# Sums of squares of two norms computed in the stages that write the residual stream, router logits with the tokens as the moving side, first expert weight splits behind the routing steps

## The reference

```
# first block
h = modulate(rmsnorm(x, norm_mix), sh1, sc1)
x = x + g1 * diff_attention(h, ...)            # ends in  o @ attn_w_out
h = modulate(rmsnorm(x, norm_ffn), sh2, sc2)   # norm 1 of the change
x = x + g2 * hier_moe(h, ...)
x = rmsnorm(x, norm_final)                     # norm 2 of the change
# second block: p = x @ w_in_2, forgetting attention, rwkv mixing, layer norms, PEER experts
```

## Time and profile before

| | us |
|---|---|
| median of 3 runs (lowest, highest) | 2693.97 (2692.8, 2698.87) |
| the profiled execution's own time | 2691.04 |
| its span | 2689.3 |
| busy PE / PEld | 2396.6 (89%) / 1788.0 (66%) |
| busy DVE / ACT / POOL | 1857.1 (69%) / 1045.6 (39%) / 708.1 (26%) |
| TensorE clock granted, mean over the span | 0.944 |

### The profile page before, as it was taken

The page is one execution under the profiler, slowest core; times in us unless marked ns, Lnnn a source line. Parts: engine busy times, 40 slices in busy tenths (PEclk is TensorE's granted clock), DMA queues, the critical chain, the costliest instruction groups (busy, mean ns, idle before and its releaser), DMA issues. The chain is left out here.

```text
span 2689.3 us, 34854 instructions
## 1 busy us (share of the span) xinstructions
PE 2396.6 (89%) x13046; PEld 1788.0 (66%) x13046; DVE 1857.1 (69%) x3303; ACT 1045.6 (39%) x1886; POOL 708.1 (26%) x648
## 2 busy tenths in 40 slices
PE   3999866999996999985889899999999999999991
PEld 2885555888885686653786688887988874444440
DVE  5639554898895322667656369998899976666669
ACT  3238644878874323653114222113877700000000
POOL 0000001213121000030000013445667766444444
PEclk7999977999998998997989999999999999999995
DMA  7943035786874132222003179798999999999997
GB/s 267 292 132 143 26 131 231 294 313 262 317 287 188 48 94 63 59 67 70 3 3 124 56 255 329 266 325 322 404 409 407 405 397 409 409 409 410 409 409 299
DMA packets 242854, 655.37 MB, mean 244 GB/s; under 512 B 25472, under 2 KB 107648, under 8 KB 227200
## 3 DMA queue, kind: packets, MB, share of 16 engines
q1 hardware_dynamic: 160608, 376.28, 38.3%
q0 software_dynamic: 82080, 276.88, 26.6%
HBM read 662.50 MB, written 34.60 MB: 259 GB/s over the span
## 5 line engine op out<-in xcount | busy, mean ns | idle before, releaser
L2658 POOL DMA_INDIRECT sp_rows<-in_u_rows,sp_flat x184 | 225.7, 1227 | 566.2 <-DVE sp_flat L3100 388.5
L285 DVE TENSOR_TENSOR wide_low<-wide_raw,wide_high 128x2048 fp32r<-128x2048 f32 x138 | 312.4, 2290 | 63.9 <-ACT wide_high L278 62.0
L2864 PE MATMUL ps<-raw,tb_made 128*128 128x512 f32 x768 | 335.0, 592 | 0.0
L2834 PE MATMUL ps<-xT,raw 128*128 128x256 f32 x1424 | 319.7, 381 | 0.0
L2834 PEld LDWEIGHTS ps<-xT,raw 128*128 128x128 f32 x1424 | 268.3, 191 | 34.8
L171 DVE TENSOR_TENSOR w_low<-raw,w_high 128x1024 fp32r<-128x1024 f32 x90 | 110.1, 1225 | 249.1 <-ACT w_high L162 248.7
L278 ACT CAST wide_high<-wide_raw 128x2048 fp32r<-128x2048 f32 x138 | 261.6, 1914 | 22.3 <-PE ps L335 16.0
L2864 PEld LDWEIGHTS ps<-raw,tb_made 128*128 128x128 f32 x768 | 145.8, 190 | 183.2 <-issue 183.2
L2667 DVE SCALAR_TENSOR_TENSOR sp_rows<-sp_rows,sp_x 128x1024 f32<-128x1024 f32 x184 | 222.9, 1223 | 21.5 <-DMA sp_rows<-in_u_rows,sp_flat 19.9
L2676 DVE SCALAR_TENSOR_TENSOR sp_x<-sp_rows,sp_coef,sp_x 128x1024 f32<-128x1024 f32 x124 | 158.4, 1286 | 81.3 <-DMA sp_rows<-in_v,sp_flat 79.8
L3000 ACT ACTIVATE pe_root<-pe_root 128x1 f32<-128x1 f32 x4 | 0.8, 203 | 490.2 <-DVE pe_root L3210 490.2
(11 more groups left out here) (522 smaller groups left out, 5151.8 us busy)
## 6 DMA issues: line engine op xcount, KB each, us to landing
wide_raw<-in_w_experts SPq DMA_DIRECT2D x96, 1024.0 KB, 6.8
raw<-in_v SPq DMA_DIRECT2D x96, 512.0 KB, 6.8
raw<-in_u SPq DMA_DIRECT2D x89, 512.0 KB, 6.8
ada_raw<-in_ada_w SPq DMA_DIRECT2D x24, 1024.0 KB, 7.4
raw<-in_w_in SPq DMA_DIRECT2D x42, 512.0 KB, 3.8
raw<-in_peer_w_q SPq DMA_DIRECT2D x32, 512.0 KB, 4.4
tb_ring<-in_v SPq DMA_DIRECT2D x32, 512.0 KB, 6.8
tb_ring<-in_u SPq DMA_DIRECT2D x29, 512.0 KB, 6.8
```

Source lines behind the costliest of these rows:

```text
L285: self.m.nc.vector.tensor_tensor(self.low_of[:, n % self.READY, :], self.raw[:, n % self.RAW, :], self.high_of[:, n % self.READY, :].bitca ...
L2658: self.m.nc.gpsimd.indirect_dma_start(out=self.rows(g), out_offset=None, in_=src, in_offset=bass.IndirectOffsetOnAxis(ap=self.flat[:, tile ...
L2834: last = nc.tensor.matmul(m.ps[:, HID + r % 2, 0:DT], u[:, c, :], m.xT[:, c, 0:DT], start=c == 0, stop=c == KT - 1)
L2864: last = nc.tensor.matmul(m.ps[:, Y + 2 * n + half, :], made[:, r, n * P:(n + 1) * P], v[:, half * T:(half + 1) * T], start=False, stop=r ...
```

## The change

- The squares of `norm_ffn` are made in `head_norm_projection`: after each chunk, ACT squares the new stream tile into `sq`, DVE adds it to the running sum, and PE makes the one product with ones behind the last projection product. DVE's scale and ACT's Ln and Exp (into `m.rstd`) stand at the end of the same block. For the last chunk, ACT squares before it writes its high weight part.
- `rms_norm` for `norm_ffn` is replaced by `ffn_norm`: DVE scales, ACT shifts, and PE multiplies each finished tile with the 20 columns of `router_w` as weights and the 512 tokens as the moving side (8 products instead of 32). ACT copies the logits, [20, 512], to SBUF.
- In `router`, PE turns the logits with 4 transposes instead of computing them. The three splits of expert weights stand behind the routing steps on ACT and DVE, not ahead.
- The squares of `norm_final` are made in `combine`: ACT squares each tile behind DVE's addition, PE sums the eight with ones, and the steps to `m.rstd` follow there. The block `inverse_rms` is gone.

```diff
@@ -543,32 +543,6 @@
                 rest(KT - 1)
 
 
-def inverse_rms(nc, m, name, out):
...
 def project(nc, m, pe, name, high, low, bank_free, chunks=8, n0=0, banks=8):
 
 
@@ -822,6 +796,8 @@
 
     squared, summed, logged, rooted, chain_s, scaled, highs, lows = (m.sem("hn_" + n) for n in (
         "squared", "summed", "logged", "rooted", "chain", "scaled", "highs", "lows"))
+    residual, x_squared, x_added, x_summed, averaged, x_rooted = (m.sem("hn_" + n) for n in (
+        "residual", "x_squared", "x_added", "x_summed", "averaged", "x_rooted"))
     with nc.Block() as block, ExitStack() as mem:
         sb = lambda n, s: mem.enter_context(nc.sbuf_tensor("hn_" + n, s, F32))
         sq, gain, eps = sb("sq", [P, HEADS, T]), sb("gain", [P, 1]), sb("eps", [P, 1])
@@ -853,6 +829,8 @@
                 w = weights(n)
                 for c in range(KT):
                     product(w, n, c)
+            pe.wait_ge(x_added, KT - 1)
+            nc.tensor.matmul(m.ps[:, 0, :], m.ones[:], sq[:, 0, :], start=True, stop=True).then_inc(x_summed, 1)
 
         @block.scalar
         def _(act):
@@ -874,9 +852,19 @@
                 if h >= 1:
                     rounded(h - 1)
             rounded(HEADS - 1)
-            for n in range(KT):
+
+            def square(n):
+                act.wait_ge(residual, n + 1)
+                nc.scalar.activation(sq[:, n, :], m.xT[:, n, :], ACT.Square).then_inc(x_squared, 1)
+
+            for n in range(KT - 1):
                 m.stream.done(act, "attn_out", n)
                 m.stream.high(act, "attn_out", n)
+                square(n)
+            square(KT - 1)
+            m.stream.high(act, "attn_out", KT - 1)
+            act.wait_ge(averaged, 1)
+            inverse_root(nc, act, m.rstd[:], x_rooted, 0)
 
         @block.vector
         def _(dve):
@@ -896,12 +884,54 @@
                 if h >= 1:
                     rest(h - 1)
             rest(HEADS - 1)
+
+            def add_square(n):
+                dve.wait_ge(x_squared, n + 1)
+                if n >= 2:
+                    dve.wait_ge(x_added, n - 1)
+                nc.vector.tensor_tensor(sq[:, 0, :], sq[:, 0, :], sq[:, n, :], ALU.add).then_inc(x_added, 1)
+
             for n in range(KT):
                 m.stream.done(dve, "attn_out", n)
                 nc.vector.scalar_tensor_tensor(out=m.xT[:, n, :], in0=m.ps[:, n, :],
                                                scalar=m.mod[:, 2 * KT + n:2 * KT + n + 1], in1=m.xT[:, n, :],
-                                               op0=ALU.mult, op1=ALU.add)
-                m.stream.low(dve, "attn_out", n)
+                                               op0=ALU.mult, op1=ALU.add).then_inc(residual, 1)
+                if n < KT - 1:
+                    m.stream.low(dve, "attn_out", n)
+                if n >= 1:
+                    add_square(n)
+            m.stream.low(dve, "attn_out", KT - 1)
+            dve.wait_ge(x_summed, 1)
+            nc.vector.tensor_scalar(m.rstd[:], m.ps[:, 0, :], 1.0 / D, EPS, ALU.mult, ALU.add).then_inc(averaged, 1)
+
+
+def ffn_norm(nc, m, h, logits):
+
+
+    scaled, shifted, summed = (m.sem("fn_" + n) for n in ("scaled", "shifted", "summed"))
+    with nc.Block() as block:
+        @block.vector
+        def _(dve):
+            for k in range(KT):
+                nc.vector.scalar_tensor_tensor(out=h[:, k, :], in0=m.xT[:, k, :], scalar=m.norm2[:, k:k + 1], in1=m.rstd[:],
+                                               op0=ALU.mult, op1=ALU.mult).then_inc(scaled, 1)
+
+        @block.scalar
+        def _(act):
+            for k in range(KT):
+                act.wait_ge(scaled, k + 1)
+                nc.scalar.activation(h[:, k, :], h[:, k, :], ACT.Identity, bias=m.mod[:, 3 * KT + k:3 * KT + k + 1]
+                                     ).then_inc(shifted, 1)
+            act.wait_ge(summed, 1)
+            nc.scalar.copy(logits[:], m.ps[0:logits.shape[0], 0, :])
+
+        @block.tensor
+        def _(pe):
+            for k in range(KT):
+                pe.wait_ge(shifted, k + 1)
+                last = nc.tensor.matmul(m.ps[0:logits.shape[0], 0, :], m.router_w[:, k, :], h[:, k, :], start=k == 0,
+                                        stop=k == KT - 1)
+            last.then_inc(summed, 1)
 
 
 def first_of_equals(nc, link, out, eq, seen, width):
@@ -912,7 +942,7 @@
     link(nc.vector.scalar_tensor_tensor(out=out, in0=seen[:], scalar=0.5, in1=eq, op0=ALU.is_lt, op1=ALU.mult))
 
 
-def router(nc, m, wide, h, rows, pos, chosen, gains, xbuf):
+def router(nc, m, wide, h, logits, rows, pos, chosen, gains, xbuf):
 
 
 
@@ -971,10 +1001,8 @@
         @block.tensor
         def _(pe):
             for tt in range(TT):
-                for c in range(KT):
-                    last = nc.tensor.matmul(m.ps[:, tt, 0:G + EXPERTS], h[:, c, tt * P:(tt + 1) * P],
-                                            m.router_w[:, c, :], start=c == 0, stop=c == KT - 1)
-                last.then_inc(logits_done, 1)
+                nc.tensor.transpose(m.ps[:, tt, 0:G + EXPERTS], logits[:, tt * P:(tt + 1) * P],
+                                    m.ident[0:G + EXPERTS, 0:G + EXPERTS]).then_inc(logits_done, 1)
             for tt in range(TT):
                 if tt >= 2:
                     pe.wait_ge(row_read, tt - 1)
@@ -996,8 +1024,6 @@
 
         @block.scalar
         def _(act):
-            for n in range(wide.READY):
-                wide.high(act, n)
             act.wait_ge(exps, 1)
             nc.scalar.activation(gx[:], gx[:], ACT.Exp).then_inc(exps, 1)
             for tt in range(2):
@@ -1010,11 +1036,11 @@
                 act.wait_ge(row_turned, tt + 1)
                 nc.scalar.copy(rows[:, tt, :], m.ps[:, 4 + 2 * (tt % 2):6 + 2 * (tt % 2), :].rearrange("p a f -> p (a f)")
                                ).then_inc(row_read, 1)
+            for n in range(wide.READY):
+                wide.high(act, n)
 
         @block.vector
         def _(dve):
-            for n in range(wide.READY):
-                wide.low(dve, n)
             link = Chain(dve, chain_s)
             bc = lambda t, n: t[:].to_broadcast([P, TT, n])
             for tt in range(TT):
@@ -1085,6 +1111,8 @@
             link(nc.vector.reciprocal(w1[:], w1[:]))
             link(nc.vector.tensor_tensor(gains[:, 0], w1[:], gs[:], ALU.mult))
             link(nc.vector.tensor_tensor(gains[:, 1], ge[:], gains[:, 0], ALU.mult))
+            for n in range(wide.READY):
+                wide.low(dve, n)
 
 
 def experts(nc, m, wide, chosen, xbuf, ybuf):
@@ -1310,11 +1338,12 @@
 def combine(nc, m, pos, gains, ybuf):
 
 
-    scaled, summed, turned, added = (m.sem("co_" + n) for n in ("scaled", "summed", "turned", "added"))
+    scaled, summed, turned, added, squared, totalled, averaged, rooted = (m.sem("co_" + n) for n in (
+        "scaled", "summed", "turned", "added", "squared", "totalled", "averaged", "rooted"))
     fetched = [m.keep_sem(f"co_fetched{tt}") for tt in range(TT)]
     with nc.Block() as block, ExitStack() as mem:
         sb = lambda n, s: mem.enter_context(nc.sbuf_tensor("co_" + n, s, F32))
-        ys, part = sb("ys", [P, TT, 2, D]), sb("part", [P, TT, D])
+        ys, part, sq = sb("ys", [P, TT, 2, D]), sb("part", [P, TT, D]), sb("sq", [P, KT, T])
 
         @block.gpsimd
         def _(pool):
@@ -1330,6 +1359,11 @@
             for tt in range(TT):
                 act.wait_ge(fetched[tt], 32)
                 nc.scalar.activation(part[:, tt, :], ys[:, tt, 0, :], ACT.Copy, scale=gains[:, 0, tt, :]).then_inc(scaled, 1)
+            for k in range(KT):
+                act.wait_ge(added, k + 1)
+                nc.scalar.activation(sq[:, k, :], m.xT[:, k, :], ACT.Square).then_inc(squared, 1)
+            act.wait_ge(averaged, 1)
+            inverse_root(nc, act, m.rstd[:], rooted, 0)
 
         @block.vector
         def _(dve):
@@ -1342,6 +1376,8 @@
                 nc.vector.scalar_tensor_tensor(out=m.xT[:, k, :], in0=m.ps[:, k, :],
                                                scalar=m.mod[:, 5 * KT + k:5 * KT + k + 1], in1=m.xT[:, k, :],
                                                op0=ALU.mult, op1=ALU.add).then_inc(added, 1)
+            dve.wait_ge(totalled, 1)
+            nc.vector.tensor_scalar(m.rstd[:], m.ps[:, 0, :], 1.0 / D, EPS, ALU.mult, ALU.add).then_inc(averaged, 1)
 
         @block.tensor
         def _(pe):
@@ -1351,6 +1387,10 @@
                     ins = nc.tensor.transpose(m.ps[:, k, tt * P:(tt + 1) * P], part[:, tt, k * P:(k + 1) * P], m.ident[:])
                     if tt == TT - 1:
                         ins.then_inc(turned, 1)
+            for k in range(KT):
+                pe.wait_ge(squared, k + 1)
+                last = nc.tensor.matmul(m.ps[:, 0, :], m.ones[:], sq[:, k, :], start=k == 0, stop=k == KT - 1)
+            last.then_inc(totalled, 1)
 
 
 def second_projection(nc, m, gain, high, low, fq, fk, fv, cols, negc, cq):
@@ -3341,8 +3381,9 @@
                         with ExitStack() as normed:
```

(25 more changed lines are left out.)

## The result

The changed kernel takes 2677.87 us (median of five executions), the kernel before beside it 2692.80. One of the five was slow, 3646.21 us at a mean granted clock of 0.643 where the others had 0.946 or 0.947; the other four took 2673.51 to 2678.76, median 2677.25, and the ratio uses these alone. It is 0.9942 [0.9929, 0.9954], so 15.6 us faster (12.4 to 19.1). Forecast: 2674.0, 20.0 faster, range 2668 to 2682: the time lies in the range, the gain of 20.0 just outside the interval. Two later sets of executions of the same kernel gave 0.9951 [0.9937, 0.9964] and 0.9944 [0.9931, 0.9958]. The profiled execution took 2678.76 us, its span is 2677.0, its mean clock 0.947.

A forecast was written before the change was run, and what follows sets the result against it. PE stands 21.6 us until scattered rows return, engines working one after another; a smaller serial place follows at norm_final. 15.9 - 3.1 + 7.2 = 20.0 us off 2691.04 gives 2671.0, plus 2.9 for the median: 2674.0; range 2668 to 2682.

The forecast's parts named there:

- Squares in the projection: Output projection: PE's stream covers seven norm_ffn squares and additions; DVE's scale step 7.9 us earlier, scaling 7.5 us earlier.
- Logits: `ffn_norm` and router: logits products take 9.2 us instead of 13.81; gain up to their read, squares included, 15.9 us.
- No delay at the ranks: Router, the routing chain's visit to PE: the 32 transposes of `h` cause no delay; bound 1.3 us.
- Scatter: Scatter of rows: each of DVE's low parts holds one POOL issue; ends 3.1 us later, bounds 0 and 6.1.
- rival A: Scatter: POOL is not held by DVE; 23.1 us gained, 2671 us; chance 12%.
- rival B: Scatter: POOL is shut out through all three splits; 17 us gained, 2677 us; chance 9%.
- Combine: Combine: squares of norm_final made behind DVE's additions; next block 7.2 us earlier, bounds 4.8 and 8.5.
- Rigid shift of the rest: Everything behind these stages: held to them by block ends and shifts as a whole, 0 us.
- rival D: Experts: start 19 us nearer a busy PE, products run long at low clock; slower, 2706 after 160 products; chance 2%.
- rival C: Clock stays low through `ffn_norm`, holds the transposes, falls in combine; 12 us gained, about 2682 us; chance 14%.

The follow-up runs named there:

- Run 8: Changed kernel plus three extra 512-column PE products between the turned rows and the rank products; 2671.57 us, ratio 0.9934 to the kernel before.
- run 4: Changed kernel with the three expert weight splits ahead of the routing steps again; 2685.18 us, ratio 0.9983 to the kernel before.
- run 6: Changed kernel with the logits computed in the router block with tokens as weights again; 2681.18 us, ratio 0.9973 to the kernel before.
- run 9: Changed kernel with each of the three low parts made by eight 256-column instructions instead of one; 2673.25 us, ratio 0.9931 to the kernel before.
- run 10: Changed kernel with weight loads and first split in `ffn_norm`, other two low parts in DVE's wait for the ranks; 2671.82 us, ratio 0.9933.
- run 11: Changed kernel with run 8's and run 10's edits together, but the third low part behind the routing steps; 2669.57 us, ratio 0.9930.
- run 12: As run 11, plus two 512-column PE products at the start of the experts; 2671.41 us, ratio 0.9926 to the kernel before.

## Why the prediction was right, and where its sizes were off

- **Squares in the projection** (7.9 at DVE's scale step, 7.5 at the first tile scaled): right, for the reason given. The three traces have 8.1, 7.7 and 8.1 at the scale step and 7.9, 7.5 and 7.9 at the tile. DVE's starts on the last two chunks lie 5.61 us apart before and after, so PE's stream covers seven of eight squares and additions. The one product took 1.13, 1.76 and 1.12: that the full clock lasts until it is done, as I had it, came true in two of three.
- **Logits** (15.9 - 7.5 = 8.4 more to their first read): right; 9.0, 8.8 and 9.2. The products took 8.71, 8.84 and 8.52 instead of 9.2, at the two spacings I had taken from norm_final's 512-column rows, so the 20 columns of weights indeed did not matter.
- **No delay at the ranks** (0): wrong, 2.3. I looked for the danger in PE being late with its 32 transposes (bound 1.3). It was early: at the full clock they ended at 378.6, PE idled 2.8 us, the level fell, and 22 small instructions took 4.85 instead of 2.6. Before, the transposes had begun at the low level, which rose during them, and ended 1.7 us ahead of the picks. Run 8 shows that work in that gap keeps the level; runs 4 and 6, slow after 1.15 and 0.8 us of idling, show that the length of the gap alone doesn't decide it.
- **Scatter** (3.1): right in size (3.07 in all three) and mechanism: one issue per low part is held until that instruction ends (runs 9 and 10). Both bounds fall, no hold (rival A) and the shut-out over all three splits (rival B). With rival A falls the hold of 0 that I had drawn from the inference of the Trainium skill (SBUF — State Buffer, "Who interferes with whom"), that tensor_tensor leaves descriptor generation alone. Which step of an issue is the one that waits, no run here shows.
- **Combine** (7.2): mechanism right, size 6.9, 4.9 and 5.1. I had taken the level of one trace, low until 867.96 and then full. It came out so in 7 of 11 profiles, and that the first was among them is luck; in the others the ones products began at the low level, which the prediction had as its bound (4.8).
- **Rigid shift of the rest** (0): the experts lost 1.0 to 1.3. Of their first weight products 11 or 12 were 0.43 apart, before 8, which is 0.6 to 0.8 of it. This is rival D's mechanism in small, and its counterargument, that the experts' own activity decides, does not hold: that activity is the same and the rise came 5.0 to 5.4 us after the first weight product, before 3.8.

Of 20.0 us the ranks take 2.3, combine about 1.5 and the experts 1.1, and the logits give 0.8: 15.9, and 15.6, 13.2 and 15.1 were measured. So the miss of four microseconds is one term that was put at nothing without a bound on the early side, and two that depend on the clock. The kernel did not get slower as D had it; of rival C, the clock, a share came true, at the ranks and in combine instead of at the logits. One reading in the prediction is off and nothing hangs on it: DVE starts on the last chunk 0.75 us before 355.11, not 1.3.

## What to carry to other kernels

When two engines keep a third from its next step and end together, only both removals earn anything; try each alone and you discard both. Work moved off a chain lands beside something: ask what it holds up there (here POOL's issues, by DVE instructions with two SBUF inputs), and break it into short instructions if it must stay. An engine that becomes early may idle, and a forecast of no delay has to be bounded on that side too: here TensorE's level fell, and its next small products took nearly twice as long. And a stage whose time hangs on the level of the clock should be read from several profiles: one trace misjudged combine by 2 us and the total by 4.

## What the runs showed of the hardware

- A POOL indirect transfer issued during a DVE subtraction with both inputs in SBUF (0.95 alone) lasts until that instruction's end and about 0.85 more (0.84 in runs 11 and 12, 0.86 in the earlier trace rows): 1.88 to 2.72 with 2.29 us instructions, 1.02 to 1.19 with pieces of 0.34, though DVE never paused.
- With PE idle from 378.6 the granted clock was at the level of 1.2 GHz from about 381.4 on; 22 instructions of 16 or 64 columns then took 4.85 instead of 2.6 us, 1.9 times as long. In run 6 it fell at about 388.8, with PE at work since 387.4 after an idle time of only 0.8.
- The same eight ones products in the same place took 7.13 to 9.13 us in different executions, and the start of one attention 9.3 to 13.2.
- A float32 product of [512 x 1024] by [1024 x 20] took 13.81 us with the 20 columns moving (64 instructions, low level) and 8.52 to 8.84 with the 512 tokens moving (16 instructions, low level at first, then full). At the low level alone the 16 would take about 13.7 (an estimate from their 0.85 an instruction there), so what the form gains in the products' own time comes with the rise of the level.
